# Mixture-of-experts results weighted and summed by TensorE with diagonal matrices, and the next layer's first weight load behind the first gather

## What is computed

```python
def run_layer(x, silu_cond, lw, rope, ctx):
    sh1, sc1, g1, sh2, sc2, g2 = modulation(silu_cond, lw['w_mod'], lw['b_mod'])
    out, ctx_tensors = token_mixer(modulate(x, lw['norm1'], sh1, sc1), lw, rope, ctx)
    x = x + g1 * out
    x = x + g2 * moe_ffn(modulate(x, lw['norm2'], sh2, sc2), lw)
...
    # in moe_ffn: the two best experts of each token, weights w normalised over the two
    w = w / jnp.sum(w, axis=-1, keepdims=True)
    gates = jnp.sum(jax.nn.one_hot(idx, N_EXPERTS, dtype=F32) * w[..., None], axis=1)
    act = jax.nn.silu(jnp.einsum('nd,edf->nef', xt, lw['w_gate'])) * jnp.einsum('nd,edf->nef', xt, lw['w_up'])
    y = jnp.einsum('nef,efd->nd', act * gates[..., None].astype(act.dtype), lw['w_down'])
```

## Time and profile before

| | |
|---|---|
| device time, median of 3 runs | 1435.25 us (1432.86 to 1435.38) |
| the profiled execution's own time | 1432.73 us |
| its span in the profile | 1430.9 us |
| mean granted clock of TensorE in it | 0.979 of full speed |
| TensorE busy | 1298.1 us, 91% of the span |
| VectorE, ScalarE, GpSimd busy | 35%, 22%, 18% |

### The profile page before, as it was taken

One profiled execution on the slowest core, in us unless ns is written; L12 is line 12 of the kernel. 1 busy time (PEld: TensorE's weight loads), 2 busy tenths in 40 slices (PEclk: granted clock), 3 DMA queues, 4 the chain that ended last, 5 costly groups with the idle time before them and its releaser, 6 DMA issues.

```text
span 1430.9 us, 17501 instructions
## 1 busy us (share of the span) xinstructions
PE 1298.1 (91%) x6833; PEld 742.8 (52%) x6834; DVE 496.8 (35%) x881; ACT 318.8 (22%) x489; POOL 259.0 (18%) x225
## 2 busy tenths in 40 slices
PE   6999999999999969889879999999999999998773
PEld 3555446675546535445536554555655554554431
DVE  2325427862145101111154353577413531110104
ACT  2136416631001100000021562464100110000001
POOL 2730017821000100000128000684200010000001
PEclk9999999999999979999989999999999999999998
DMA  9897426654437999999974231576442579999996
GB/s 348 259 344 265 177 84 230 220 192 148 176 117 296 355 380 386 387 396 391 415 255 138 69 112 59 175 242 238 163 176 118 216 278 366 367 387 386 408 416 261
DMA packets 117049, 371.85 MB, mean 260 GB/s; under 512 B 18016, under 2 KB 33024, under 8 KB 100336
## 3 DMA queue, kind: packets, MB, share of 16 engines
q1 hardware_dynamic: 86496, 329.69, 61.1%
q0 software_dynamic: 6480, 21.95, 4.2%
q10 hardware_dynamic: 24000, 19.21, 4.2%
HBM read 341.40 MB, written 29.43 MB: 259 GB/s over the span
## 4 chain that ended last, share of the span: by engine, by line
PE 72%; DMA 14%; DVE 8%; issue 2%; ACT 2%; SPq 1%; ACTq 0%; POOL 0%; DVEq 0%
PE pG L1749 24%; PE pS L1838 11%; PE pG L1741 10%; PE pG L1994 6%; PE pG L1856 6%; DMA ring<-in_w_exp_up_dram 6%; DMA modb<-in_w_exp_up_dram 3%; PE pX L1679 3%; PE pX L1838 2%; DMA hT_gen<-x_scr 2%; PE pG L1712 2%; DMA ring<-in_w_mod_dram 2%; PE pS L1780 1%; DVE ring L1326 1%; PE pX L1804 1%
## 5 line engine op out<-in xcount | busy, mean ns | idle before, releaser
L1749 PE MATMUL pG<-hT_gen,ring 128*128 128x384 f32 x1024 | 339.6, 489 | 1.6 <-ACT hT_gen L1061 1.6
L1749 PEld LDWEIGHTS pG<-hT_gen,ring 128*128 128x128 f32 x1024 | 191.8, 190 | 141.5 <-issue 13.7
L1838 PE MATMUL pS<-ring,hT_gen 128*64 128x256 f32 x1344 | 155.9, 388 | 15.7 <-DMA ring<-in_w_exp_up_dram 6.8
L1741 PE MATMUL pG<-ring,hT_gen 128*128 128x512 f32 (+1 forms) x384 | 150.8, 549 | 5.1 <-ACT hT_gen L928 2.9
L1838 PEld LDWEIGHTS pS<-ring,hT_gen 128*64 128x64 f32 x1344 | 104.7, 140 | 69.3 <-issue 14.6
L1614 DVE TENSOR_TENSOR hT_gen<-pS,hT_gen 128x256 f32<-128x256 f32 x32 | 19.2, 601 | 329.6 <-PE pS L1838 329.6
L1741 PEld LDWEIGHTS pG<-ring,hT_gen 128*128 128x128 f32 x384 | 72.3, 192 | 74.8 <-issue 68.3
L820 POOL DMA_INDIRECT ring<-y_scr,idx x12 | 11.4, 946 | 483.7 <-ACTq L1138 480.7
L1856 PE MATMUL pG<-ring,hT_gen 128*64 128x512 f32 x352 | 82.4, 610 | 11.5 <-DVE hT_gen L1617 8.8
L708 POOL TENSOR_TENSOR stat<-stat,half 128x1 f32<-128x1 f32 (+3 forms) x30 | 28.7, 956 | 310.1 <-DVE stat L1279 209.9
L1994 PE MATMUL pG<-ring,hT_gen 128*128 128x512 f32 x192 | 83.1, 592 | 0.0
(11 more groups left out here) (302 smaller groups left out, 1638.8 us busy)
## 6 DMA issues: line engine op xcount, KB each, us to landing
ring<-in_w_mod_dram SPq DMA_DIRECT2D x24, 2048.0 KB, 8.6
ring<-in_w_exp_up_dram SPq DMA_DIRECT2D x22, 2048.0 KB, 25.4
ring<-in_w_in_dram SPq DMA_DIRECT2D x20, 2048.0 KB, 8.8
ring<-in_w_exp_down_dram SPq DMA_DIRECT2D x20, 2048.0 KB, 24.4
ring<-in_w_exp_gate_dram SPq DMA_DIRECT2D x20, 2048.0 KB, 24.6
modb<-in_w_exp_up_dram SPq DMA_DIRECT2D x10, 2048.0 KB, 30.2
hT_gen<-in_w_exp_down_dram SPq DMA_DIRECT2D x10, 2048.0 KB, 29.7
rows_nw<-in_w_exp_gate_dram SPq DMA_DIRECT2D x10, 2048.0 KB, 30.3
```

The source lines that it names most:

```text
L1741: ins = pe.matmul(ps[:, 0:width], hT[:, k, t * P:(t + 1) * P], w[:, k, 0:width], start=(k == 0), stop=(k == KC - 1))
L1749: ins = pe.matmul(ps[:, 0:TOK], w[:, k, c0:c0 + P], src[:, k, :], start=(k == 0), stop=(k == nk - 1))
L1838: ins = pe.matmul(dst[64 * hf:64 * hf + 64, 0:256], x[:, k, :], w[k][:, 256 * hf:256 * (hf + 1)], start=(k == 0), stop=(k == KC - 1))
```

## The change

The weights become matrices. While expert 15 runs, VectorE makes six 128 by 128 diagonal matrices (identity times a column of `wgt`), two for each tile, once the last store out of `ysb[1]` has landed, because three of them lie there. TensorE leaves the accumulation of the one-hot products open and adds, for each tile and each half of 512 columns, diagonal 0 times the first gathered row and diagonal 1 times the second: 12 products of 128 rows by 512 columns a layer. ScalarE's scaling and VectorE's `pair` and `last_added` go; VectorE's work is now `gated` and `into_x` in halves of 512 columns, straight from PSUM. `IDLE_TURN` becomes 1. SyncE issues the next layer's `q` load only when tile 0's two gathers have landed.

```diff
-IDLE_TURN = 7
+IDLE_TURN = 1
...
-        last_y = xT01.rearrange("p e k s -> p (e k s)")
+        y_gated = xT01.rearrange("p e k s -> p (e k s)")
+        diag = [[xrow[2][:, P * t:P * (t + 1)] for t in range(NT)], [ysb[1][:, P * t:P * (t + 1)] for t in range(NT)]]
...
                         if n == 0:
                             sp.wait_ge(e_down, L * NE - 2)
                             further_done(NE - 3)
+                            sp.wait_ge(yg_in[0], 32 * L)
...
-            def scale_y(L, t):
-
-                act.wait_ge(yg_in[t], 32 * (L + 1))
-                y0 = results[:, t, 0, :]
-                act.activation(y0, y0, ACT.Identity, scale=wgt[:, 0, t:t + 1]).then_inc(y_scaled, 1)
-
...
                 act.copy(ysb[0], bank[1]).then_inc(e_y, 1)
-                for t in range(NT):
-                    scale_y(L, t)
...
-            def pair(L, t):
-                y0, y1 = results[:, t, 0, :], results[:, t, 1, :]
-                dve.wait_ge(yg_in[t], 32 * (L + 1))
-                dve.wait_ge(y_scaled, NT * L + t + 1)
-                link(dve.scalar_tensor_tensor(y0, y1, wgt[:, 1, t:t + 1], y0, ALU.mult, ALU.add))
...
-            def last_added(L, t, hf):
-                y0 = results[:, t, 0, 512 * hf:512 * (hf + 1)]
-                dve.wait_ge(last_out, NT * L + t + 1)
-                link(dve.tensor_tensor(y0, bank[2 + 2 * t + hf], y0, ALU.add))
-
-            def combine_first(L):
+            def gated(L, t, hf):
+                half = slice(512 * hf, 512 * (hf + 1))
                 dve.wait_ge(gate2_in, 16 * 2 * (L + 1))
...
+                dve.wait_ge(y_sum, 2 * NT * L + 2 * t + hf + 1)
+                link(dve.tensor_tensor(y_gated[:, half], bank[2 + 2 * t + hf], modb[:, 2, min(t, 1), half], ALU.mult))
+
+            def into_x(t, hf):
+                half = slice(512 * hf, 512 * (hf + 1))
+                ins = dve.tensor_tensor(xs[:, t, half], xs[:, t, half], y_gated[:, half], ALU.add)
+                if hf == 1:
+                    ins.then_inc(x_done, 1)
+
+            def combine(L, t):
                 for hf in range(2):
...
+                    gated(L, t, hf)
+                    into_x(t, hf)
...
                 further_blocks(NE - 1, xT[1])
+                dve.wait_ge(e_ydma[1], 32 * YS[1] * (L + 1) + YB[1])
+                for c in range(2):
+                    for t in range(NT):
+                        ins = dve.tensor_scalar(diag[c][t], ident, wgt[:, c, t:t + 1], None, ALU.mult)
+                ins.then_inc(diag_ready, 1)
                 activated(L * NE + NE - 1)
...
                     for t in range(NT):
                         for u in range(2):
-                            ins = pe.matmul(bank[2 + 2 * t + u], lastP[64 * u:64 * u + 64, t, :],
-                                            ysb[0][64 * u:64 * u + 64, :], start=True, stop=True)
-                        ins.then_inc(last_out, 1)
+                            pe.matmul(bank[2 + 2 * t + u], lastP[64 * u:64 * u + 64, t, :],
+                                      ysb[0][64 * u:64 * u + 64, :], start=True, stop=False)
+                    pe.wait_ge(diag_ready, L + 1)
+                    for t in range(NT):
+                        pe.wait_ge(yg_in[t], 32 * (L + 1))
+                        for u in range(2):
+                            for i in range(2):
+                                ins = pe.matmul(bank[2 + 2 * t + u], diag[i][t], results[:, t, i, 512 * u:512 * (u + 1)],
+                                                start=False, stop=(i == 1))
+                            ins.then_inc(y_sum, 1)
```

More of the change, by code:

```diff
@@ L341, in build @@
         mc_evac = sem("mc_evac")
-        y_scaled = sem("y_scaled")
         mods_in = sem("mods_in")
@@ L441, in build @@
         last_weights = sem("last_weights")
-        last_out = sem("last_out")
+        diag_ready = sem("diag_ready")
+        y_sum = sem("y_sum")
         x_done = sem("x_done")
@@ L1244, in norm1_out @@
                 ins.then_inc(hT_v, 1)
-            def pair(L, t):
-                y0, y1 = results[:, t, 0, :], results[:, t, 1, :]
-                dve.wait_ge(yg_in[t], 32 * (L + 1))
-                dve.wait_ge(y_scaled, NT * L + t + 1)
-                link(dve.scalar_tensor_tensor(y0, y1, wgt[:, 1, t:t + 1], y0, ALU.mult, ALU.add))
[L1252 to L1257, removed]
-            def last_added(L, t, hf):
-                y0 = results[:, t, 0, 512 * hf:512 * (hf + 1)]
-                dve.wait_ge(last_out, NT * L + t + 1)
-                link(dve.tensor_tensor(y0, bank[2 + 2 * t + hf], y0, ALU.add))
-            def combine_first(L):
-                dve.wait_ge(gate2_in, 16 * 2 * (L + 1))
-                dve.wait_ge(last_out, NT * L + 1)
-                for hf in range(2):
[L1268 to L1275, removed]
+            def gated(L, t, hf):
+                half = slice(512 * hf, 512 * (hf + 1))
+                dve.wait_ge(gate2_in, 16 * 2 * (L + 1))
+                dve.wait_ge(y_sum, 2 * NT * L + 2 * t + hf + 1)
[6 more added lines that the diff above has]
+            def combine(L, t):
+                for hf in range(2):
+                    gated(L, t, hf)
+                    into_x(t, hf)
             def norm2(L, t):
@@ L1374, in _ @@
                 else:
-                    combine_first(L - 1)
+                    combine(L - 1, 0)
                     norm1_mean(L, 0)
-                    last_added(L - 1, 1, 0)
                     norm1_rows(L, 0)
-                    last_added(L - 1, 1, 1)
                     dve.wait_ge(mc_evac, MOD_FIRST * (L + 1))
+                    combine(L - 1, 1)
                     norm1_out(L, 0)
[L1382 to L1386, removed]
                     norm1_mean(L, 1)
-                    gated(2)
                     norm1_rows(L, 1)
-                    into_x(2, results[:, 2, 0, :]).then_inc(x_done, 1)
+                    combine(L - 1, 2)
+                    norm1_out(L, 1)
                     norm1_mean(L, 2)
-                    norm1_out(L, 1)
                     norm1_rows(L, 2)
@@ L1661, in _ @@
                 further_blocks(NE - 1, xT[1])
-                activated(L * NE + NE - 1)
[L1664 to L1671, removed]
+                dve.wait_ge(e_ydma[1], 32 * YS[1] * (L + 1) + YB[1])
[3 more added lines that the diff above has]
+                ins.then_inc(diag_ready, 1)
+                activated(L * NE + NE - 1)
+            for t in range(NT):
+                combine(DEPTH - 1, t)
         @block.tensor
```

## The result

| | before | after |
|---|---|---|
| device time, median of 5 runs | 1434.61 us (1432.86 to 1435.38) | 1425.17 us (1424.0 to 1433.1) |
| ratio after / before | | 0.9947, 95% interval [0.9929, 0.9966] |
| forecast | | 1427.0 us (1424.0 to 1431.5) |

What follows compares the result with a forecast made beforehand. TensorE, busy 91% of the span, was taken as the bound, so only its waits and the work after its last product could be won. 4.1 + 2.95 = 7.05 us off 1434.06 gave 1427.0 us, range 1424.0 to 1431.5.

Steps and rivals of the forecast that it cites:

- Unit prices: Instruction costs: 0.897 us per diagonal product, 0.65 for `gated` and 0.61 for `into_x` on 512 columns.
- The first gather: Between the layers: with the q load held back, tile 0 lands at 717.8, 6.0 us after issue, just where TensorE comes free.
- The collision: Between layers, q load slows tile 2's gathers: landing 725.2, in time; rival 727.7, products 2.15 us late, 1429.2 us, chance 0.15.
- The load itself: The q load between the layers: 10 to 11 us from issue to landing, needed 14.3 us after issue, no cost.
- q's start and its second tile: Between the layers: q starts 2.7 us earlier (732.15 against 734.81), its second tile 4.1 us earlier (741.2 against 745.28).
- The clock: TensorE between the layers: granted clock near 1.00 from 725 to 740 us, no longer falling; some 2 us of the 4.1.
- The end: After the last layer's one-hot products: finish at 1424.87 against 1427.82, 2.95 us less, VectorE only following TensorE.
- A gain that is given back: Second layer's experts: if DMA queues set that layer's end, only the end's 2.95 us remain, 1431.1 us; chance 0.08.
- the distance stays: From the second q tile on, both kernels are bound by TensorE, so the 4.1 us won there is kept.
- The sum: Whole kernel: 4.1 us between the layers plus 2.95 at the end, 7.05 us off 1434.06, giving 1427.0 us.

Runs made afterwards that it cites:

- e6: The change with the q load held behind the third gather instead of the first: 1425.64 us, ratio 0.9957 to the kernel before.
- e11: The change run a third time without edit, beside e8's kernel on one chip: 1427.23 us, ratio 0.9953 to the kernel before.
- e7: The change between the layers, with the old sum on ScalarE and VectorE at the end of the last layer: 1429.61 us, ratio 0.9985.
- neutral relatives: The kernel before with an already met wait ahead of the q load (1433.26 us), and with one unused product instead of seven (1434.31 us).
- e3: The kernel before with only the q load held back behind the first gather: 1433.01 us against 1432.34 beside it, ratio 1.0004.
- e8: The change with tile 0's transposes ahead of tile 2's products and no unused product between the layers: 1423.74 us, ratio 0.9945.
- e9: The kernel before with one more, already met, wait on SyncE ahead of the q load: 1433.26 us against 1434.09, ratio 0.9994.
- e5: The kernel before run again without edit, for a second trace of it: 1431.5 us once.

## Why the prediction was right, point by point

- **Unit prices.** 0.897 us a product: 3.6 to 3.7 us for four. `gated` and `into_x` on 512 columns took 0.69 us each, not 0.65 and 0.61, which did not matter, as VectorE follows TensorE. The six diagonal instructions took 1.26 us instead of 1.7 and lay in VectorE's rest (6.79 us of it left in the trace of the change).
- **The first gather.** Forecast 717.8, that is 3.0 us after S1; 3.0 in the second trace of the change (716.91 against 713.87), 3.5 in the third, and 6.3 before.
- **The collision.** I put it at 0.2 us and gave its rival 0.15. TensorE waited 0.91 and 1.07 us for tile 2's gather in two traces of the change and not at all in e6, where the load comes later: half a rival. In these two the term was mis-sized by some 0.8 us. In the third (e11) TensorE did not wait there, but 0.62 us for tile 0's gather:

```profile
721.11 3.67 PE L2084 MATMUL pS<-ring,hT_gen 128*128 128x512 f32 x8 [0.62 <-DMA ring<-y_scr,idx]
```

  The working had two faults. The rival's landing was 727.7, but its lateness of 2.15 us was taken from 727.15, 0.5 us too little. And the reading that `q` had half of the bytes from 712.6 to 724.0 in the old trace was wrong: the gathers' queue (q0) moved 3.02 MB there and that of the weights (q1) 1.30:

```profile
q0 software_dynamic: 827, 3.02, 66.5%
q1 hardware_dynamic: 652, 1.30, 30.9%
```

  So the old trace does not show that the two share equally. The trace of the change comes near it: `q`'s first packets move over 3 us after its issue at 720.0, and from 724 to 726 us q0 moves 0.44 MB and q1 0.34. The last gather takes 8.9 us there; in e6, where the load comes later, no gather takes over 7.2. The load itself took 11.7 to 12.9 us, not 10 to 11; 14.3 were forecast as its time, and in the first two traces it had 15.6 and 15.4. e6 shows what more lateness does.
- **q's start and its second tile.** Forecast 2.7 and 4.1 us earlier relative to S1. `q` starts 17.9, 18.3 and 17.5 us after S1 in the three traces against 20.0, so 1.7 to 2.5 earlier; the waits for the gathers took the rest. The stage as a whole is 4.6 us shorter: GpSimd's power took 0.54 us instead of the 1.45 I allowed for, so tile 1 caught up. A term 0.5 us too small.
- **The clock.** Forecast near 1.00 from 725 to 740; 1.00 in each stretch.
- **The end.** 2.95 us forecast, 3.1 measured, and e7 gives 3.0 back by undoing it alone.
- **A gain that is given back.** I gave it 0.08 and looked for it in the experts' weight loads. G2-S2 does not show it beyond its scatter (259.4 to 261.3 in four traces of the old kernel and its neutral relatives, 261.0 to 262.0 in three of the change; the means differ by 1.2 us, which I leave open). It was in T-G2, 2.8 us in the traces, where I had written that from the second `q` tile on the distance stays. That step was wrong.
- **The sum.** 7.05 us forecast. The two stages gave 7.7 and T-G2 took 2.8; the three ratios of the change (0.9947, 0.9959, 0.9953) say 7.6, 5.9 and 6.7 us of about 1434. The stages of the traces leave 4.9 of the 7.7, less than any of the three ratios says; since the traced executions of the change were slower than its medians, either the others lose less in T-G2 or scatter covers the difference, and this stays open. The total came out right partly by luck: the gain was a little larger than forecast and a loss was not foreseen, and the intervals, 1.9 to 2.7 us to either side, would not tell.

## What to carry to other kernels

A sum that follows transfers belongs on the engine that waits for its result, if that engine would rest anyway: it needs the same wait, saves two engines' queues, and keeps the clock up where unused products did not. When a transfer is brought forward, first look which of a group the consumer really waits for; the old kernel waited for the last gather, so it won the 1.5 us by which the last one came sooner, not the 4 expected from the first (e3). A gain at one place should be checked stage by stage to the end, since in the traces 2.8 of 7.7 us were lost again 240 us later at a wait for a 16 KB transfer.

## What the runs showed of the hardware

- The time that a stop costs TensorE depends on more than its length. After waits of 4.3 to 4.4 us at the same instruction the granted clock of the next 8 us was 0.63 in the change and 0.80 in e8, a difference of 1.7 us in T-G2, and after 2.93 us in e9 it stayed at 1.00, while after 2.95 us in e5 it was 0.81. Even so e9's T-G2 was only 0.3 us shorter, as TensorE at the higher clock met a wait of 0.77 us for VectorE.
- The `q` load of 2 MB took 7.8 us from issue to landing behind all gathers (e6) and 11.7 to 12.9 us beside four remaining gathers of 0.5 MB each (the three traces of the change).
